# Second recurrent layer: score levels joined four blocks at a time, products of 192 columns

## The chip, the cores and the metric

The kernel runs on one core of a Trainium2 chip. The metric is the device time of one execution in microseconds (us), lower is better; the time of a kernel is the median of its runs.

## What is computed

Two transformer blocks over 256 tokens of width 1024. The first block has two layers, a gated delta rule layer and then the HGRN2 layer that this case is about; the second block is a sliding-window attention with an MLP. The HGRN2 layer, cut to its core (16 heads of 128 features, chunks of 32 tokens in the reference):

```
q_raw, f_raw, i_in, z = split(x @ w_in, 4)
f = lower_bound + (1 - lower_bound) * sigmoid(f_raw);  q = silu(q_raw);  k = 1 - f;  logf = log(f)
b = cumsum(logf)                                       # inside a chunk
attn[t, s] = sum_d q[t, d] * k[s, d] * exp(b[t, d] - b[s, d])        for s <= t
o_t  = (q_t * exp(b_t)) @ state + attn @ v
state = state * exp(b_last) + (k * exp(b_last - b))^T @ v
out = (rms_norm(o) * silu(z)) @ w_out
```

So the score of a query t and a key s is a sum over features of q times k times the product of the forget gates f between the two tokens. Everything is float32 in and out.

## The kernel before

**Dense products.** The weights are streamed in units of 512 KB: SyncE loads a unit into `raw`, ScalarE rounds it to the high half (`whi`, L1042), GpSimd subtracts to get the low half (`wlo`, L468 and L469), and TensorE multiplies high by high, high by low and low by high (`three`, L489; lines L492, L493 and L494). In the HGRN2 layer a unit is one call of `wide_unit` (24 matmuls of 256 columns). Two units each make the forget gates, the queries, the values and the output gates of a pair of heads, so that a pair takes eight units, and the eight pairs 64.

**Steps.** Each engine runs its own copy of the loop `for g in range(HG_STEPS)`, one unit to a step, the first 64 steps for the eight pairs and ten more in which the units of the output projection are multiplied. What belongs to pair p is done at fixed offsets r = g - 8 p: its four kinds of projections at r = 0 to 7, its scores at r = 4 to 12, its output at r = 13 to 17. So at g = 8 p + 5, for one, pair p begins its scores while pair p - 1 (r = 13) makes its outputs. Within a step TensorE first multiplies the unit, then does the score work, then the product across the tile halves, the output product (`hg_out`) and the sum of squares (L892, at r = 15, behind a wait on `hg_yg`). The order is written out by hand, and an engine does its instructions in that order; there is no scheduler.

**Scores.** A tile has 128 tokens; two heads times two tiles make four score tiles (u = 0 to 3). Level s (1, 2, 4, 8, 16, 32, 64) takes the pairs of neighbouring blocks of s tokens: queries in the odd block, keys in the even one. The queries and keys lie in `QK`. The queries start as q times f (`hg_gate`, L1905). For each level:

- TensorE (`hg_levels`, L829) multiplies all 128 keys of a tile by the 64 queries in odd blocks, four matmuls of 64 columns (L846). A float32 matmul is two instructions in the trace, so they are 8 records. At level 1 four matmuls of 128 columns with the plain queries are added (L844), for the diagonal.
- VectorE (`level`, L1908) waits for these, multiplies queries and keys by the decays of the next level in one instruction of 512 elements (L1913), picks the blocks that belong to this level out of PSUM into the score tile `AA` by a masked copy of 256 elements (L1921, COPY_PREDICATED; at level 1 a copy of the diagonal too, L1918), and halves the list of decays by a reduction (L1924).

Level k of pair p is at r = 4 + k. At r = 12 come two matmuls of 128 columns across the two tiles (L855) and their copy to `CR` (L1940); at r = 13 `hg_out` (L868 to L870); at r = 14 ScalarE squares the outputs (L1378) and VectorE then multiplies them by norm gain and gate into `yg` (L1945); at r = 15 TensorE sums the squares (L892). ScalarE turns them into a root at r = 16, and VectorE finishes at r = 16 and 17.

On VectorE `yg` of pair p - 1 stands in the same step (g = 8 p + 6) behind level 2 of pair p; every linked instruction of VectorE waits for the one before it to end (`link`, `settle`).

The loop on VectorE, and what it calls at r = 5 to 14:

```
for p in range(HH // 2):
    r = g - 8 * p
    if r == 4:
        hg_gate(p)
    if 5 <= r < 12:
        level(p, r - 4)
...
    if r == 14:
        vec.wait_ge(hg_sq, p + 1)
```

Of the kernel before, what the change touches and what calls it, by code (L numbers as in the profile page):

```python
# [5 lines left out]
F32 = mybir.dt.float32  # L6
# [6 lines left out]
P = 128  # L13
# [26 lines left out]
C_DIST = C_PICK + len(LEVELS) * P // 2  # L40
# [11 lines left out]
HG_STEPS = 4 * HH + SKEW  # L52
FIRST_YA = 4 * GH
# [83 lines left out]
def build(nc, a, consts, out):  # L137
    with ExitStack() as ctx:
# [34 lines left out]
        pick = {s: con[:, C_PICK + 64 * i:C_PICK + 64 * (i + 1)].bitcast(I32) for i, s in enumerate(LEVELS)}  # L173
# [29 lines left out]
        with ExitStack() as ph:  # L203
            fth = sb("fth", [P, 2 * T], stack=ph)
            q0 = sb("q0", [P, 2, 2 * T], stack=ph)
            QK = sb("QK", [P, 2, 2, 2 * T], stack=ph)
# [34 lines left out]
        SB = [ctx.enter_context(nc.psum_tensor(f"bank{i}", [P, 512], F32)) for i in range(4)]  # L241
# [86 lines left out]
        hg_gated = sem("hg_gated")  # L328
        hg_level_mm = sem("hg_level_mm")
        hg_level = sem("hg_level")  # L330
# [150 lines left out]
        def _(pe):  # L481
# [328 lines left out]
            def hg_unit(par, which, i, t):  # L810
                return QK[:, par, which, i * T + t * P:i * T + (t + 1) * P]

# [16 lines left out]
            def hg_levels(p, k):  # L829

                par, s = p % 2, LEVELS[k - 1]
                if k == 1:
                    pe.wait_ge(hg_gated, p + 1)
                    if p > 0:
                        pe.wait_ge(hg_cross, p)
                        pe.wait_ge(hg_picked, 7 * p)
                else:
                    pe.wait_ge(hg_level, 7 * p + k - 1)
                    pe.wait_ge(hg_picked, 7 * p + max(k - 2, 1))
                for i in range(2):  # L840
                    for t in range(NT):
                        u = 2 * i + t
                        if k == 1:
                            pe.matmul(SB[0][:, u * P:(u + 1) * P], hg_unit(par, 1, i, t), q0[:, par, i * T + t * P:i * T + (t + 1) * P],  # L844
                                      start=True, stop=True)
                        last = pe.matmul(SB[k % 2][:, u * 64:(u + 1) * 64], hg_unit(par, 1, i, t), even_odd(hg_unit(par, 0, i, t), s, 1),  # L846
                                         start=True, stop=True)
                last.then_inc(hg_level_mm, 1)

            def hg_across(p):  # L850

                pe.wait_ge(hg_level, 7 * p + 7)
# [1263 lines left out]
```

## Time and profile before

| | before |
|---|---|
| median of 3 runs | 1030.72 us (1030.56 to 1031.1) |
| the profiled execution | 1031.01 us |
| its span in the trace | 1029.2 us, 18128 instructions |
| TensorE busy | 987.0 us (96%), 7200 matmul records |
| VectorE, ScalarE, GpSimd busy | 424.4, 502.9 and 669.4 us |
| granted TensorE clock, mean | 0.993 |

The span is 1.8 us shorter than the time of the same execution; the rest lies outside the trace. Busy shares are of the whole span. A matmul record's duration contains the pipeline through the array, so that the records of a row overlap: what a matmul costs is the distance from its start to the next one's start. Engine names: PE is TensorE, PEld its weight loads, DVE VectorE, ACT ScalarE, POOL GpSimd.

### The profile page before, as it was taken

What the parts mean: (1) busy time and instruction counts of PE and PEld (TensorE: products, weight loads), DVE (VectorE), ACT (ScalarE), POOL (GpSimd) and SP (SyncE); (2) the same over time, 40 slices, a digit from 0 to 9 for tenths busy, and PEclk for the clock granted to TensorE, in tenths of its full rate; (3) what the DMA queues carried; (4) which work ended last, traced back from release to release, by engine and by line L of the source; (5) the groups of instructions that cost most, each with busy time, mean ns of one, the idle gap of its engine ahead of it and who ended that gap; (6) DMA issues with size and microseconds to landing.
All of it is one profiled execution on the core that took longest, in us unless ns stands there. A gap on an engine that the chain in (4) does not pass through costs nothing.

```text
span 1029.2 us, 18128 instructions
## 1 busy us (share of the span) xinstructions
PE 987.0 (96%) x7200; PEld 924.1 (90%) x7200; DVE 424.4 (41%) x748; ACT 502.9 (49%) x705; POOL 669.4 (65%) x476
## 2 busy tenths in 40 slices
PE   4999999999999999999999999999997989999996
PEld 4899999999998889999999999888886779998884
DVE  2457653376433342444444444425557262221003
ACT  3675332573225556454465545456636625654330
POOL 3995535466444797855665666659673369889981
PEclk9999999999999999999999999999998999999998
DMA  7989757759523565644444444455552046656631
GB/s 186 213 197 130 133 100 83 143 103 106 126 98 123 174 204 166 182 123 128 139 124 124 124 142 133 131 179 174 171 168 62 20 145 203 190 182 190 204 119 41
DMA packets 131100, 146.23 MB, mean 142 GB/s; under 512 B 11006, under 2 KB 95688, under 8 KB 131016
## 3 DMA queue, kind: packets, MB, share of 16 engines
q1 hardware_dynamic: 127448, 140.06, 52.8%
q10 hardware_dynamic: 3568, 5.01, 1.5%
q8 instruction: 57, 0.93, 0.4%
q14 instruction: 27, 0.22, 0.1%
HBM read 144.00 MB, written 1.05 MB: 141 GB/s over the span
## 4 chain that ended last, share of the span: by engine, by line
PE 84%; DVE 5%; POOL 3%; issue 3%; DMA 3%; ACT 2%; SPq 1%; DVEq 0%; ACTq 0%; POOLq 0%
PE dense L492 21%; PE dense L494 21%; PE dense L493 21%; PE bank L846 4%; DMA raw<-in_w_in_even_dram 3%; PE bank L750 2%; PE bank L745 2%; POOL wlo L469 2%; PE bank L749 2%; POOL wlo L468 1%; PE bank L844 1%; PE bank L961 1%; PE bank L892 1%; PE dense L561 1%; DVE cv L1604 1%
## 5 line engine op out<-in xcount | busy, mean ns | idle before, releaser
L468 POOL TENSOR_TENSOR wlo<-raw,whi 128x512 fp32r<-128x512 f32 x200 | 260.2, 1301 | 287.9 <-ACT whi L1042 287.7
L1042 ACT ACTIVATE whi<-raw 128x1024 fp32r<-128x1024 f32 x264 | 276.4, 1058 | 327.2 <-PE dense L494 272.3
L469 POOL TENSOR_TENSOR wlo<-raw,whi 128x512 fp32r<-128x512 f32 (+1 forms) x264 | 412.6, 1570 | 27.9 <-ACT whi L1042 27.7
L492 PE MATMUL dense<-x_hi,whi 128*128 128x256 f32 x1232 | 360.9, 293 | 6.9 <-POOL wlo L469 2.3
L494 PE MATMUL dense<-x_hi,wlo 128*128 128x256 f32 x1232 | 349.1, 283 | 0.0
L493 PE MATMUL dense<-x_lo,whi 128*128 128x256 f32 x1232 | 349.1, 283 | 0.0
L492 PEld LDWEIGHTS dense<-x_hi,whi 128*128 128x128 f32 x1232 | 236.9, 192 | 11.1 <-issue 4.6
L493 PEld LDWEIGHTS dense<-x_lo,whi 128*128 128x128 f32 x1232 | 236.9, 192 | 1.8 <-issue 1.7
L494 PEld LDWEIGHTS dense<-x_hi,wlo 128*128 128x128 f32 x1232 | 236.4, 192 | 0.0
L492 PE MATMUL dense<-whi,ya_hi 128*128 128x512 f32 x192 | 77.7, 405 | 0.7 <-DVE ya_lo L2024 0.7
L494 PE MATMUL dense<-whi,ya_lo 128*128 128x512 f32 x192 | 75.0, 390 | 0.0
L493 PE MATMUL dense<-wlo,ya_hi 128*128 128x512 f32 x192 | 74.9, 390 | 0.0
L1913 DVE TENSOR_TENSOR QK<-QK,bank 128x512 f32<-128x512 f32 x48 | 33.0, 688 | 94.8 <-PE bank L846 94.8
L846 PE MATMUL bank<-QK 128*128 128x64 f32 x448 | 58.8, 265 | 0.0
L846 PEld LDWEIGHTS bank<-QK 128*128 128x128 f32 x448 | 57.1, 192 | 0.3
L1032 ACT ACT_TABLE_LOAD x32 | 41.1, 1283 | 6.3 <-issue 4.6
L1604 DVE SCALAR_TENSOR_TENSOR cv<-dense,colA,cv 128x255 f32<-128x255 f32 (+2 forms) x72 | 34.7, 481 | 22.8 <-ACT cv L1123 20.3
L492 PEld LDWEIGHTS dense<-whi,ya_hi 128*128 128x128 f32 x192 | 36.1, 188 | 8.6 <-DVE ya_lo L2024 1.1
L494 PEld LDWEIGHTS dense<-whi,ya_lo 128*128 128x128 f32 x192 | 36.0, 188 | 7.8
L493 PEld LDWEIGHTS dense<-wlo,ya_hi 128*128 128x128 f32 x192 | 36.2, 188 | 7.2 <-issue 0.5
L492 PE MATMUL dense<-whi,x_hi 128*128 128x256 f32 (+1 forms) x144 | 40.9, 284 | 0.0
L493 PE MATMUL dense<-wlo,x_hi 128*128 128x256 f32 (+1 forms) x144 | 40.6, 282 | 0.0
(294 smaller groups left out, 1471.6 us busy)
## 6 DMA issues: line engine op xcount, KB each, us to landing
raw<-in_w_in_odd_dram SPq DMA_DIRECT2D x64, 512.0 KB, 3.7
raw<-in_w_in_even_dram SPq DMA_DIRECT2D x32, 512.0 KB, 10.7
raw<-in_w_in_even_dram SPq DMA_DIRECT2D x64, 256.0 KB, 4.6
raw<-in_mlp_w_up_dram SPq DMA_DIRECT2D x32, 512.0 KB, 4.0
raw<-in_mlp_w_down_dram SPq DMA_DIRECT2D x32, 512.0 KB, 4.7
raw<-in_w_out_even_dram SPq DMA_DIRECT2D x16, 512.0 KB, 3.7
raw<-in_w_pl_gate_dram SPq DMA_DIRECT2D x16, 512.0 KB, 4.5
raw<-in_w_out_odd_dram SPq DMA_DIRECT2D x16, 512.0 KB, 3.8
```

The costliest lines, as they stand in the source:

```text
L468: pool.tensor_tensor(wlo[:, slot, 0:half], unit_slot(u)[:, 0:half], whi[:, slot, 0:half].bitcast(F32), ALU.subtract)
L469: pool.tensor_tensor(wlo[:, slot, first:2 * half], unit_slot(u)[:, first:2 * half], whi[:, slot, first:2 * half].bitcast(F32), ALU.subtrac ...
L492: pe.matmul(out_, lh, rh, start=start, stop=False, skip_group_check=True)
L493: pe.matmul(out_, lh, rl_, start=False, stop=False, skip_group_check=True)
L494: return pe.matmul(out_, ll, rh, start=False, stop=stop, skip_group_check=True)
L745: last = pe.matmul(A[:, o], unit(LT[:, g, :], u), unit(XN[:, g, :], u), start=True, stop=True)
L749: pe.matmul(B[:, u * 64:(u + 1) * 64], unit(XT[:, g, :], u), even_odd(unit(EL[:, g, :], u), lv, 0), start=True, stop=True)
L846: last = pe.matmul(SB[k % 2][:, u * 64:(u + 1) * 64], hg_unit(par, 1, i, t), even_odd(hg_unit(par, 0, i, t), s, 1), start=True, stop=True)
L1032: act.preload_act_table_set(name)
L1042: act.activation(whi[:, u % NSPL, :], unit_slot(u), ACT.Copy).then_inc(hi_done, 1)
L1604: link(vec.scalar_tensor_tensor(o, bank[:, i * T:(i + 1) * T - back], colA[:, w:w + 1], o, ALU.mult, ALU.add), conv_done if back == 3 else ...
L1913: vec.tensor_tensor(qk, qk, both_decays(p, s), ALU.mult).then_inc(hg_level, 1)
```

## The change

The blocks are joined four at a time instead of two at a time. For s = 1, 4 and 16 (`HG_BLOCKS`, at r = 6, 8 and 10) four neighbouring blocks of s tokens become one of 4 s. Six block pairs lie within four blocks; each needs its own decay on the query. `hw` holds, for each group of four, eight columns of blocks, of which the middle six are the right-hand side of one matmul of 192 columns (`hg_blocks`). So a pair of heads has four matmuls of 128 columns for the diagonal (r = 5), three times four of 192 (r = 6, 8, 10) and four of 64 for the halves (r = 11). The matmuls of r = 7 and r = 9 are gone. Banks 0 and 1 of PSUM become one tensor `bank01`.

On VectorE a block stage has ten instructions (six at s = 16), where each of two levels had a product, a pick and a reduction: the queries for the next stage (384 elements, then 256 and 128 for the extra variants, `hg_variants`), the keys (256 elements twice), and three picks of 384, 256 and 128 elements, each with a mask of runs of 3 s, 2 s and s out of 6 s; then two reductions. ScalarE gets a copy of 128 elements three times for each pair (`hg_move`). The mask table is 192 columns wider. Below are the added lines; what they replace (`hg_levels`, `level`, `both`, `both_decays`) stands in the listing above.

```
+HG_BLOCKS = (6, 8, 10)
...
+        pick = {s: con[:, C_PICK + 192 * i:C_PICK + 192 * (i + 1)].bitcast(I32) for i, s in enumerate((1, 4, 16))}
+        pick_half = con[:, C_PICK + 3 * 192:C_DIST].bitcast(I32)
...
+            def hg_diagonal(p):
+                pe.wait_ge(hg_q, p + 1)
+                if p > 0:
+                    pe.wait_ge(hg_cross, p)
+                for u in range(4):
+                    last = pe.matmul(SB[0][:, u * P:(u + 1) * P], tokens_of(hk, p % 2, u // 2, u % 2), tokens_of(q0, p % 2, u // 2, u % 2),
+                                     start=True, stop=True)
+                last.then_inc(hg_level_mm, 1)
+            def hg_blocks(p, n):
+                s = 4 ** n
+                pe.wait_ge(hg_ranked, 5 * p + n + 1)
+                pe.wait_ge(hg_picked, 5 * p + n + 1)
+                for u in range(4):
+                    six = hw[:, n % 2, u * T:(u + 1) * T].rearrange("p (m c) -> p m c", c=8 * s)[:, :, s:7 * s]
+                    last = pe.matmul(low_banks[:, u * T:u * T + 192], tokens_of(hk, p % 2, u // 2, u % 2), six, start=True, stop=True)
+                last.then_inc(hg_level_mm, 1)
+            def hg_halves(p):
+                pe.wait_ge(hg_ranked, 5 * p + 4)
+                pe.wait_ge(hg_picked, 5 * p + 4)
+                for u in range(4):
+                    last = pe.matmul(SB[0][:, u * 64:(u + 1) * 64], tokens_of(hk, p % 2, u // 2, u % 2), tokens_of(q0, p % 2, u // 2, u % 2)[:, 64:P],
+                                     start=True, stop=True)
+                last.then_inc(hg_level_mm, 1)
+            def hg_across(p):
+                pe.wait_ge(hg_ranked, 5 * p + 5)
+                pe.wait_ge(hg_picked, 5 * p + 5)
                 for i in range(2):
...
+                    last = pe.matmul(SB[0][:, i * P:(i + 1) * P], tokens_of(hk, p % 2, i, 0), tokens_of(q0, p % 2, i, 1), start=True, stop=True)
                 last.then_inc(hg_cross_mm, 1)
...
+            def hg_move(p, n):
+                s = 4 ** n
+                act.wait_ge(hg_ranked, 5 * p + n + 1)
+                if n > 0:
+                    act.wait_ge(hg_level_mm, 5 * p + n + 1)
+                act.activation(ranked(p, n + 1)[:, :, :, 0:s], hw[:, n % 2, :].rearrange("p (m b c) -> p m b c", b=2, c=8 * s)[:, :, :, 0:s],
+                               ACT.Copy).then_inc(hg_moved, 1)
+                settle(hg_moved)
...
+            def pairs(p, s):
+                link(vec.tensor_reduce(decays(p, 2 * s), decays(p, s).rearrange("p (n t) -> p n t", t=2), AX_X, ALU.mult))
+            def spread(f, n):
+                return f.unsqueeze(len(f.shape)).broadcast_to([*f.shape, n])
+            def hg_variants(p, n):
+                s = 4 ** n
+                eight = hw[:, n % 2, :].rearrange("p (n c r) -> p n c r", c=8, r=s)
+                f = decays(p, s).rearrange("p (n t) -> p n t", t=4)
+                next_two = hw[:, n % 2, :].rearrange("p (n h c r) -> p n h c r", h=2, c=4, r=s)[:, :, :, 2, :]
+                link(vec.tensor_tensor(next_two, eight[:, :, 4:6, :], spread(f[:, :, 1:3], s), ALU.mult))
+                return vec.tensor_tensor(eight[:, :, 3, :], eight[:, :, 6, :], spread(f[:, :, 1], s), ALU.mult)
             def hg_gate(p):
                 vec.wait_ge(hg_decay, 2 * p + 2)
                 vec.wait_ge(hg_q, p + 1)
+                link(vec.tensor_tensor(ranked(p, 0), q0[:, p % 2, :].rearrange("p (m b r) -> p m b r", b=2, r=1),
+                                       decays(p, 1).rearrange("p (m b r) -> p m b r", b=2, r=1), ALU.mult))
+                link(hg_variants(p, 0), hg_ranked)
+                pairs(p, 1)
+                pairs(p, 2)
+            def hg_diagonal(p):
+                vec.wait_ge(hg_level_mm, 5 * p + 1)
                 if p - 1 > 0:
...
+                    vec.wait_ge(hg_o, p - 1)
+                vec.copy_predicated(four(AA[:, p % 2, :]), all4(ident).bitcast(I32), four(SB[0])).then_inc(hg_picked, 1)
                 settle(hg_picked)
...
+            def hg_blocks(p, n):
+                s, par = 4 ** n, p % 2
+                f = decays(p, s).rearrange("p (m b t) -> p m b t", b=2, t=4)
+                three = hw[:, n % 2, :].rearrange("p (m b c) -> p m b c", b=2, c=8 * s)[:, :, :, s:4 * s]
+                if n > 0:
+                    vec.wait_ge(hg_level_mm, 5 * p + n + 1)
+                link(vec.tensor_tensor(ranked(p, n + 1)[:, :, :, s:4 * s], three, spread(f[:, :, :, 0], 3 * s), ALU.mult))
+                if n < 2:
+                    vec.wait_ge(hg_moved, 3 * p + n + 1)
+                    link(hg_variants(p, n + 1))
+                vec.wait_ge(hg_level_mm, 5 * p + n + 2)
+                keys = hk[:, par, :].rearrange("p (n t r) -> p n t r", t=2, r=s)[:, :, 0, :]
+                link(vec.tensor_tensor(keys, keys, spread(decays(p, s).rearrange("p (n t) -> p n t", t=2)[:, :, 1], s), ALU.mult))
+                keys = hk[:, par, :].rearrange("p (n t r) -> p n t r", t=2, r=2 * s)[:, :, 0, :]
+                if n == 2:
+                    vec.wait_ge(hg_moved, 3 * p + 3)
+                link(vec.tensor_tensor(keys, keys, spread(decays(p, 2 * s).rearrange("p (n t) -> p n t", t=2)[:, :, 1], 2 * s), ALU.mult), hg_ranked)
+                if n == 0:
                     free("qf", p)
+                a = AA[:, par, :].rearrange("p (u m c) -> p u m c", u=4, c=4 * s)
+                got = low_banks[:, :].rearrange("p (u c) -> p u c", u=4)[:, :, 0:192].rearrange("p u (m c) -> p u m c", c=6 * s)
+                mask = pick[s].rearrange("p (m c) -> p m c", c=6 * s).unsqueeze(1).broadcast_to([P, 4, 32 // s, 6 * s])
+                link(vec.copy_predicated(a[:, :, :, s:4 * s], mask[:, :, :, 0:3 * s], got[:, :, :, 0:3 * s]))
+                link(vec.copy_predicated(a[:, :, :, 2 * s:4 * s], mask[:, :, :, 3 * s:5 * s], got[:, :, :, 3 * s:5 * s]))
+                link(vec.copy_predicated(a[:, :, :, 3 * s:4 * s], mask[:, :, :, 5 * s:6 * s], got[:, :, :, 5 * s:6 * s]), hg_picked)
+                if n < 2:
+                    pairs(p, 4 * s)
+                    if n == 0:
+                        pairs(p, 8)
+                    else:
+                        pairs(p, 32)
+            def hg_halves(p):
+                par = p % 2
+                vec.wait_ge(hg_level_mm, 5 * p + 5)
+                f = decays(p, 64).rearrange("p (i t h) -> p i t h", i=2, t=2)
+                k = hk[:, par, :].rearrange("p (i c) -> p i c", i=2)[:, :, 0:64]
+                q = q0[:, par, :].rearrange("p (i c) -> p i c", i=2)[:, :, P + 64:T]
+                link(vec.tensor_tensor(k, k, spread(f[:, :, 0, 1], 64), ALU.mult))
+                link(vec.tensor_tensor(q, q, spread(f[:, :, 1, 0], 64), ALU.mult), hg_ranked)
+                o = AA[:, par, :].rearrange("p (u c) -> p u c", u=4)[:, :, 64:P]
+                link(vec.copy_predicated(o, pick_half.unsqueeze(1).broadcast_to([P, 4, 64]), SB[0][:, 0:256].rearrange("p (u c) -> p u c", u=4)), hg_picked)
```

VectorE's instructions before, from level 1 of a pair (r = 5) to the first instruction of level 3 (r = 7). `QK` are queries and keys, `AA` the score tiles, `con` the masks, `bank` PSUM:

```order
L1913 TENSOR_TENSOR QK<-QK,dense 128x2x256 [waits hg_level_mm,hg_cross]
L1918 COPY_PREDICATED AA<-con,bank 128x512 [waits hg_o,hg_level]
L1921 COPY_PREDICATED AA<-con,bank 128x256 [waits vec_chain]
L1924 TENSOR_REDUCE bank<-dense 128x256 [waits hg_picked]
L1913 TENSOR_TENSOR QK<-QK,bank 128x2x128x2 [waits vec_chain,hg_level_mm]
L1921 COPY_PREDICATED AA<-con,bank 128x128x2 [waits hg_level]
L1924 TENSOR_REDUCE bank<-bank 128x128 [waits hg_picked]
L1945 SCALAR_TENSOR_TENSOR yg<-bank,colB,szo 128x512 [waits hg_z,hg_sq,vec_chain]
L1913 TENSOR_TENSOR QK<-QK,bank 128x2x64x4 [waits hg_level_mm,hg_yg]
```

The same place in the changed program, r = 5 (its first row) and all of r = 6. `hw` are the query blocks, `hk` the keys:

```order
L1957 COPY_PREDICATED AA<-con,bank 128x512 [waits hg_o,hg_level_mm,hg_cross]
L1967 TENSOR_TENSOR hw<-hw,dense 128x64x2x3 [waits hg_picked]
L1939 TENSOR_TENSOR hw<-hw,bank 128x64x4 [waits hg_moved,vec_chain]
L1940 TENSOR_TENSOR hw<-hw,bank 128x32x4 [waits vec_chain]
L1973 TENSOR_TENSOR hk<-hk,dense 128x256 [waits hg_level_mm,vec_chain]
L1977 TENSOR_TENSOR hk<-hk,bank 128x128x2 [waits vec_chain]
L1983 COPY_PREDICATED AA<-con,bank 128x128x3 [waits hg_ranked]
L1984 COPY_PREDICATED AA<-con,bank 128x128x2 [waits vec_chain]
L1985 COPY_PREDICATED AA<-con,bank 128x128 [waits vec_chain]
L1927 TENSOR_REDUCE bank<-bank 128x64 [waits hg_picked]
L1927 TENSOR_REDUCE bank<-bank 128x32 [waits vec_chain]
L2026 SCALAR_TENSOR_TENSOR yg<-bank,colB,szo 128x512 [waits hg_z,hg_sq,vec_chain]
```

Between the wait for the matmuls (`hg_level_mm`, at L1913 before and L1973 now) and `yg` there stood three instructions; now seven stand there.

TensorE in the changed program around the same place: the score matmuls of r = 6 (pair p), the dense matmuls of the step after (`L503` to `L505`, of which the first three stand here), and the sum of squares of pair p - 1:

```order
L857 MATMUL bank<-hw,hk 128x192 [waits hg_picked,hg_ranked]
L857 MATMUL bank<-hw,hk 128x192 x3
L503 MATMUL dense<-x_hi,whi 128x256 [waits lo_done]
L504 MATMUL dense<-x_lo,whi 128x256
L505 MATMUL dense<-x_hi,wlo 128x256
...
L914 MATMUL bank<-sqo,con 128x512 [waits hg_yg]
```

Before, four matmuls of 64 columns of r = 7 stood between that dense step and the sum of squares; now it follows the dense step at once.

## Rows read from the trace of the kernel before

**Rows 1.** The page: busy time, TensorE's granted clock in 40 slices, the chain.

```profile
PE 987.0 (96%) x7200; PEld 924.1 (90%) x7200; DVE 424.4 (41%) x748; ACT 502.9 (49%) x705; POOL 669.4 (65%) x476
...
PEclk9999999999999999999999999999998999999998
...
PE 84%; DVE 5%; POOL 3%; issue 3%; DMA 3%; ACT 2%; SPq 1%; DVEq 0%; ACTq 0%; POOLq 0%
```

**Rows 2.** Stage view: us, busy (instructions) by engine, clock, DMA share, GB/s.

```profile
core 0: us, PE busy (x) PEld busy (x) DVE busy (x) ACT busy (x) POOL busy (x), PEclk, DMA share, GB/s
410.00:665.00 255.00, 255.00 (x2089) 249.35 (x2088) 113.44 (x203) 132.07 (x163) 163.71 (x130) 1.00 0.45 135
536.00:568.77 32.77, 32.77 (x278) 32.29 (x276) 14.59 (x26) 17.68 (x23) 20.30 (x16) 1.00 0.43 129
```

**Rows 3.** Waits from 405 to 665 us: who for whom, us, times, longest.

```profile
DVE QK L1913 <- PE bank L846: 127.1, 56, 4.2
POOL wlo L468 <- ACT whi L1042: 91.3, 60, 3.6
ACT sqo L1378 <- issue: 9.5, 6, 1.6
```

**Rows 4.** TensorE's timeline, r = 5 to 8 of one pair: start, duration.

```profile
538.95 0.39 PE L844 MATMUL bank<-q,QK 128*128 128x128 f32 x2
...
540.69 0.44 PE L868 MATMUL bank<-AA,vtok 128*128 128x128 f32 x2
...
542.00 0.36 PE L492 MATMUL dense<-x_hi,whi 128*128 128x256 f32 x1
...
544.95 1.00 PE L846 MATMUL bank<-QK 128*128 128x64 f32 x8
545.76 0.36 PE L492 MATMUL dense<-x_hi,whi 128*128 128x256 f32 x1
545.97 0.28 PE L493 MATMUL dense<-x_lo,whi 128*128 128x256 f32 x1
...
548.72 1.00 PE L846 MATMUL bank<-QK 128*128 128x64 f32 x8
549.56 1.08 PE L892 MATMUL bank<-sqo,con 128*128 128x512 f32 x2
550.07 0.68 PE L492 MATMUL dense<-x_hi,whi 128*128 128x256 f32 x1
550.59 0.28 PE L493 MATMUL dense<-x_lo,whi 128*128 128x256 f32 x1
```

**Rows 5.** VectorE's timeline over the same steps.

```profile
541.68 0.74 DVE L1918 COPY_PREDICATED AA<-con,bank 128x512 f32<-128x512 int32 x1
542.46 0.74 DVE L1921 COPY_PREDICATED AA<-con,bank 128x256 f32<-128x256 int32 x1
543.23 0.70 DVE L1924 TENSOR_REDUCE bank<-dense 128x256 f32<-128x512 f32 x1
545.99 0.69 DVE L1913 TENSOR_TENSOR QK<-QK,bank 128x512 f32<-128x512 f32 x1 [2.06 <-PE bank L846]
546.72 0.76 DVE L1921 COPY_PREDICATED AA<-con,bank 128x256 f32<-128x256 int32 x1
547.51 0.43 DVE L1924 TENSOR_REDUCE bank<-bank 128x128 f32<-128x256 f32 x1
547.97 0.75 DVE L1945 SCALAR_TENSOR_TENSOR yg<-bank,colB,szo 128x512 f32<-128x512 f32 x1
...
550.55 0.44 DVE L1921 COPY_PREDICATED AA<-con,bank 128x256 f32<-128x256 int32 x1
```

**Rows 6.** VectorE's groups by shape: count, busy us, mean ns.

```profile
L1998 DVE SCALAR_TENSOR_TENSOR lg<-con,dense 128x384 f32<-128x384 f32 x16 | 8.9, 553 | 8.9 <-PE dense L942 8.5
L1940 DVE COPY CR<-bank 128x256 f32<-128x256 f32 x8 | 3.4, 425 | 12.4 <-PE bank L855 12.4
L1924 DVE TENSOR_REDUCE bank<-bank 128x64 f32<-128x128 f32 x8 | 2.4, 299 | 0.3
L1924 DVE TENSOR_REDUCE bank<-bank 128x32 f32<-128x64 f32 x8 | 1.9, 232 | 0.3
```

**Rows 7.** All engines, 780 to 783 us: a stop of TensorE ended by VectorE.

```profile
780.93 1.42 DVE L1970 SCALAR_TENSOR_TENSOR qa<-dense,root 128x512 f32<-128x512 f32 x2 [0.16 <-DVE rsum L2017]
...
782.40 1.22 PE L941 MATMUL dense<-ka,qa 64*128 64x256 f32 x3 [2.91 <-DVE qa L1970]
```

**Rows 8.** ScalarE's timeline, r = 4 and r = 14.

```profile
533.08 0.58 ACT L1353 ACTIVATE q<-dense 128x512 f32<-128x512 f32 x1
...
542.33 0.60 ACT L1378 ACTIVATE sqo<-bank 128x512 f32<-128x512 f32 x1 [1.58 <-issue]
```

More of the change, by code:

```diff
@@ L240, in build @@
         DB = [[ctx.enter_context(nc.psum_tensor(f"dense{i}{j}", [P, 512], F32)) for j in range(2)] for i in range(2)]
-        SB = [ctx.enter_context(nc.psum_tensor(f"bank{i}", [P, 512], F32)) for i in range(4)]
+        low_banks = ctx.enter_context(nc.psum_tensor("bank01", [P, 1024], F32))
+        SB = [low_banks[:, 0:512], low_banks[:, 512:1024]]
+        SB += [ctx.enter_context(nc.psum_tensor(f"bank{i}", [P, 512], F32)) for i in (2, 3)]
         raw_ready = [sem(f"raw_ready{i}") for i in range(NRAW)]
@@ L327, in build @@
         hg_z = sem("hg_z")
-        hg_gated = sem("hg_gated")
+        hg_ranked = sem("hg_ranked")
+        hg_moved = sem("hg_moved")
         hg_level_mm = sem("hg_level_mm")
-        hg_level = sem("hg_level")
         hg_picked = sem("hg_picked")
@@ L807, in _, with tokens_of @@
             layer_tail(0)
-            def hg_unit(par, which, i, t):
-                return QK[:, par, which, i * T + t * P:i * T + (t + 1) * P]
+            def tokens_of(buf, par, i, t):
+                return buf[:, par, i * T + t * P:i * T + (t + 1) * P]
             def hg_dense(g):
@@ L827, in hg_dense @@
                     last.then_inc(split_used, 1)
[L829 to L847, printed above, removed]
+            def hg_diagonal(p):
[6 more added lines that the diff above has]
+                last.then_inc(hg_level_mm, 1)
@@ L853, in hg_across @@
-                pe.wait_ge(hg_picked, 7 * p + 6)
+                pe.wait_ge(hg_ranked, 5 * p + 5)
+                pe.wait_ge(hg_picked, 5 * p + 5)
                 for i in range(2):
-                    last = pe.matmul(SB[0][:, i * P:(i + 1) * P], hg_unit(p % 2, 1, i, 0), hg_unit(p % 2, 0, i, 1), start=True, stop=True)
+                    last = pe.matmul(SB[0][:, i * P:(i + 1) * P], tokens_of(hk, p % 2, i, 0), tokens_of(q0, p % 2, i, 1), start=True, stop=True)
                 last.then_inc(hg_cross_mm, 1)
@@ L1398, in _ @@
                 split_until(min(FIRST_SPLIT[("hg_f", 0, 0)] + g + 1 + AHEAD, FIRST_SPLIT[("pl", 1, 0)]))
+                for p in range(HH // 2):
+                    r = g - 8 * p
+                    if r + 1 in HG_BLOCKS:
+                        hg_move(p, HG_BLOCKS.index(r + 1))
                 for p in range(HH // 2):
@@ L1933, in _ @@
                         hg_gate(p)
-                    if 5 <= r < 12:
-                        level(p, r - 4)
+                    if r == 5:
+                        hg_diagonal(p)
+                    if r in HG_BLOCKS:
+                        hg_blocks(p, HG_BLOCKS.index(r))
+                    if r == 11:
+                        hg_halves(p)
                 for p in range(HH // 2):
@@ L2081, in shape_constants @@
         out[:, C_NEG + n * P:C_NEG + (n + 1) * P] = np.where(below, -1, 0)
-        out[:, C_PICK + n * 64:C_PICK + (n + 1) * 64] = below.T.reshape(P, P // (2 * s), 2, s)[:, :, 1, :].reshape(P, 64)
         if s == 1:
             out[:, C_NEG1T:C_NEG1T + P] = np.where(below.T, -1, 0)
+    for n, s in enumerate((1, 4, 16)):
+        same = np.arange(P)[:, None] // (4 * s) == np.arange(P // (4 * s))[None, :]
+        block = np.arange(P) // s % 4
+        rows = np.stack([block == b for b in (0, 0, 0, 1, 2, 1)], 1)
+        mask = (same[:, :, None] & rows[:, None, :])[:, :, :, None].repeat(s, 3)
+        out[:, C_PICK + 192 * n:C_PICK + 192 * (n + 1)] = mask.reshape(P, 192)
+    out[:, C_PICK + 3 * 192:C_DIST] = np.arange(P)[:, None] < 64
     key = np.arange(2 * P)[None, :]
```

47 lines of the change are left out of this document (14 added, 33 removed).

## Prediction

> **What bounds the kernel now.** I read the page first. TensorE is busy 96% of the span and makes 84% of the chain that ended last, at a granted clock of 0.9 or more of full speed in every slice [rows 1]; VectorE is busy 41%. Then I read the stretch that the change touches. From 410 to 665 us TensorE is busy for all of 255.00 us at a clock of 1.00, which is the 2.4 GHz level, while VectorE is busy for 113 [rows 2]. One pair of heads takes 32.77 us and TensorE has no gap in it [rows 2]. The waits of this stretch say the same: TensorE waits for nobody, VectorE waits 127.1 us in total for the score matmuls [rows 3]. So what TensorE no longer does comes off the end, microsecond for microsecond, as long as no wait of TensorE takes its place. Two questions decide: how much shorter is TensorE's own work, and does VectorE, now slack, stay ahead of each place where TensorE waits for it?
>
> **TensorE's own work.** Only the distance between starts is read. Level 1 with the diagonal runs from 538.95 to 540.69: 1.74 us for 8 records of 128 columns and 8 of 64. The output product that follows takes from 540.69 to 542.00, 12 records of 128 columns, 0.109 us each. So the 8 records of 64 columns cost 1.74 - 8 x 0.109 = 0.87 us. The group of level 3 takes 548.72 to 549.56, 0.84 us, where a sum of squares follows. The group of level 2 starts at 544.95; the dense matmul after it starts at 545.76 and the next at 545.97, and two dense matmuls are some 0.12 apart, so the group costs 545.97 - 544.95 - 0.12 = 0.90 us with the change of kind at its edges, which is 0.105 a record and 0.06 for the edges [rows 4].
>
> - Removed for each pair: the 64-column groups of r = 5 (0.87), of r = 7 (0.84) and of r = 9 (0.90). Sum 2.61 us.
> - Widened: the groups of r = 6, 8 and 10 from 64 to 192 columns. No row has 192. The nearest are 64 columns at 0.105, 128 at 0.109 and 512: the two records of the sum of squares cost 550.59 - 549.56 - 0.12 = 0.91 us with edges [rows 4], so 0.43 each without. From 64 to 128 columns nothing is added, and 512 costs in proportion to its columns: a record costs its columns or some 0.105, whichever is more. 192 columns then cost 192/512 x 0.43 = 0.16. Eight records are 8 x (0.16 - 0.105) = 0.44 us more, three groups 1.32. If the whole 0.455 of a 512-column record went by columns it would be 0.17 and 1.6 us.
> - The group of r = 11 keeps its size, and the diagonal and the product across the tiles keep theirs.
>
> Net 2.61 - 1.32 = 1.29 us for each pair, **10.3 us** for eight (bounds 8 and 11).
>
> **The new wait.** At g = 8 p + 7 TensorE sums the squares of pair p - 1 and must have `yg`. On VectorE `yg` stands behind all of pair p's stage at r = 6, and that stage cannot go on before the score matmuls of r = 6 are done. Before, these matmuls started at 544.95, VectorE's product followed at 545.99, and `yg` ended at 547.97 + 0.75 = 548.72; TensorE came to the sum at 549.56 [rows 4, 5]. That is 0.84 us to spare, just what the matmuls of r = 7 took. Now they are gone and the chain on VectorE is longer. With B for the start of the r = 6 matmuls:
>
> - TensorE comes to the sum at B + 0.81 (the old group, 544.95 to 545.76) + 0.44 (wider) + 2.96 (the dense step, 545.76 to 548.72) = B + 4.21 [rows 4].
> - VectorE starts its keys at B + 1.04 + 0.44 = B + 1.48 [rows 4, 5].
> - Two key products of 256 elements. 384 elements take 0.553 and a copy of 256 takes 0.425 [rows 6]; 512 take 0.69 [rows 5]. So some 0.155 plus 1.04 ns an element: 0.42 each, 0.84.
> - Three masked picks at s = 1. This is the dear part. Before, a pick of 256 elements took 0.74 at s = 1 and 0.76 at s = 2, but 0.44 at s = 4, and the diagonal's 512 elements, contiguous, took 0.74 [rows 5]. The mask and the bank were read in one piece in all of them; what differs is how broken the writing is. Counting elements, broken runs cost some 2.2 ns each and long runs 1.1. Counting groups of four neighbours in the score tile, each group touched costs 4.4 ns, whether one, two or four of it are written: 128 groups at s = 1, at s = 2 and for the diagonal, 64 at s = 4. The new picks write 3, 2 and 1 of each four. By elements they are 1.03 + 0.75 + 0.46, by groups 0.75 three times: 2.24 both ways. I take 2.24.
> - Two reductions, 0.30 + 0.23 [rows 6], then `yg`, 0.75 [rows 5].
> - Seven gaps of 0.03 between linked instructions, as between the rows of [rows 5]: 0.24.
>
> The sum is 0.84 + 2.24 + 0.53 + 0.75 + 0.24 = 4.60, so `yg` ends at B + 6.08. TensorE starts 0.05 us after VectorE's end where it waited for it elsewhere (780.93 + 1.42 to 782.40) [rows 7]. It starts the sum at B + 6.13 in place of B + 4.21, and stands still for **1.92 us**. This happens for the seven pairs that have one behind them, 13.4 us. Nothing earns it back: the next unit stands behind the sum on TensorE. The squares are not what is late: ScalarE made them from 542.33 [rows 8], long before.
>
> **What stays hidden.** TensorE's matmuls of r = 8 need the picks of r = 6, and those of r = 10 the picks of r = 8; two dense steps lie between, over 5.9 us, for chains of 4.6 us at most. From r = 10 to r = 11 there is one dense step: VectorE starts at 1.48, two key products 0.84, three picks at s = 16, where runs are long (0.59 + 0.44 + 0.31), gaps 0.13, ends at 3.79 against 4.21, so 0.4 us are to spare. At r = 4 VectorE now does the halves' three short ones, the query product, two variants and two reductions before the copy to `CR`. From ScalarE's query (533.08 + 0.58 [rows 8]), 1 us into a dense step, these are 0.69 + 0.42 + 0.29 + 0.70 + 0.43 and the copy 0.42, done 4.5 us into that step, where the diagonal needs it only after that step, the product across and the next step, over 6 us. ScalarE's three small copies a pair, no longer than the 0.6 us of its 512-element ones [rows 8], stand behind its unit copies; it is busy for 17.68 of 32.77 us [rows 2] and GpSimd, which waits for it, for 20.30. The wider mask table is loaded once, far ahead. All of this at nothing.
>
> **Sum.** -10.3 + 13.4 = +3.1 us. Against the profiled execution, 1031.01, that is 1034.1; the median of the runs shown is 0.3 lower, so I predict 1033.8.
>
> **Rivals.**
>
> - *Cheap picks.* If short runs of three and one cost what long ones do and the pair of two as well, the picks are 0.59 + 0.44 + 0.31 = 1.34, the stop is 1.02 us, seven of them 7.1, and the time is 1030.7 - 3.2 = 1027.5. Against it: 0.74 and 0.76 in every one of eight pairs at s = 1 and 2. For it: no row has three of four. Chance 0.16.
> - *Only touches of a line count.* Here a pick pays extra only where a single element of four is written: 0.59 + 0.44 + 0.74 = 1.77, the stop 1.45, seven of them 10.1, the net -0.2 and the time 1030.5. Rows speak against it, since two of four already cost 0.74 where four cost 0.44 [rows 5]. The Trainium skill (SBUF — State Buffer, section on the DMA port swizzle, its note on "cachelines") states this rule: lines of 16 bytes, full bandwidth with two or more accesses to a line, a penalty with one. By that rule the old picks at s = 1 and 2 would have been full speed; the trace disagrees with its 0.74 against 0.44. Chance 0.16.
> - *A second stop, or dear columns.* If the picks at s = 16 also cost 2.24, because their masks and banks are now read in pieces, r = 11 is late by 0.5 us in eight pairs (4 us), the first stop grows by some 0.3 (2 us) for the same reason, and 192 columns may cost the upper bound (2.3 us). This goes to slower from 0.4 us of extra on VectorE at r = 10 on; the time would be about 1040. Chance 0.12.
> - *No stop.* If VectorE were ahead after all, the 10.3 us would stand alone: 1020.4. For that, 1.9 of the 4.6 us that I count on VectorE would have to be missing, more than cheap picks can give. Chance 0.04.
>
> **How the numbers follow.** The forecast has 0.52. What a measurement of this kernel can tell from no change is about 0.2%, or 2 us. The forecast's own spread (stop 1.7 to 2.1, gain 9.5 to 10.7) is +1.2 to +5.2, of which I put 0.07 within 2 us. Slower: 0.45 + 0.12 = 0.57; same: 0.07 + 0.16 = 0.23; faster: 0.16 + 0.04 = 0.20. The range goes from the cheap picks to just short of the second stop: 1027 to 1038.5, which leaves out the case without a stop and most of the last but one.
>
> **What would show it.** In the changed profile TensorE should wait for VectorE's `yg` seven times, some 1.9 us each, and for nothing else between 405 and 665 us. A group of eight 192-column records should take some 1.3 us to the next dense matmul. The picks at s = 1 should add up to 2.2 us, those at s = 4 and 16 to 1.3. The period of a pair should be 32.77 - 1.29 + 1.92 = 33.4 us. The prediction is wrong if that wait is missing or below 1.4 us, or if TensorE stops at r = 11.

## The result

The changed kernel took 1040.7 us (median of 6 runs, 1035.2 to 1043.3) beside 1030.6 us for the kernel before; the ratio is 1.0088, 95% interval 1.0064 to 1.0111. Measured once more, beside the experiments below, it was 1038.9 us beside 1030.5, ratio 1.0075 (1.0059 to 1.0091). So it is slower by some 8 to 10 us. I had forecast slower by 3 us and a range up to 1038.5. The profiled execution took 1039.84 us, its span is 1038.0 us.

Waits from 400 to 680 us in the changed kernel (who waits for whom, us in total, times, longest). Before, TensorE stood in no row of this stretch [rows 3]:

```profile
DVE hk L1973 <- PE bank L857: 73.0, 24, 5.7
...
PE bank L914 <- DVE yg L2026: 14.0, 7, 2.0
ACT L1054 <- PE bank L914: 11.6, 7, 2.4
DVE hk L2000 <- PE bank L865: 11.2, 8, 1.7
```

TensorE's timeline over r = 6 and 7 of one pair, the counterpart of [rows 4], start and duration:

```profile
514.27 1.47 PE L857 MATMUL bank<-hw,hk 128*128 128x192 f32 x8
515.44 0.41 PE L503 MATMUL dense<-x_hi,whi 128*128 128x256 f32 x1
...
518.32 0.28 PE L505 MATMUL dense<-x_hi,wlo 128*128 128x256 f32 x1
520.59 1.12 PE L914 MATMUL bank<-sqo,con 128*128 128x512 f32 x2 [1.99 <-DVE yg L2026]
521.15 0.68 PE L503 MATMUL dense<-x_hi,whi 128*128 128x256 f32 x1
```

VectorE's timeline over the same time, the counterpart of [rows 5]:

```profile
515.84 0.42 DVE L1973 TENSOR_TENSOR hk<-hk,dense 128x256 f32<-128x256 f32 x1 [3.42 <-PE bank L857]
516.30 0.42 DVE L1977 TENSOR_TENSOR hk<-hk,bank 128x256 f32<-128x256 f32 x1
516.87 0.75 DVE L1983 COPY_PREDICATED AA<-con,bank 128x384 f32<-128x384 int32 x1
517.65 0.74 DVE L1984 COPY_PREDICATED AA<-con,bank 128x256 f32<-128x256 int32 x1
518.43 0.72 DVE L1985 COPY_PREDICATED AA<-con,bank 128x128 f32<-128x128 int32 x1
519.18 0.56 DVE L1927 TENSOR_REDUCE bank<-bank 128x64 f32<-128x128 f32 x2
519.78 0.75 DVE L2026 SCALAR_TENSOR_TENSOR yg<-bank,colB,szo 128x512 f32<-128x512 f32 x1
```

This is the wait that the prediction named, at its place and seven times, 2.00 us each. VectorE starts 1.57 us after the matmuls, `yg` ends 6.26 us after them, and TensorE starts the sum 0.06 us later. The three picks take 0.75, 0.74 and 0.72 us for 384, 256 and 128 elements.

What the prediction did not have shows in the granted clock. Two pairs in the view by stages (us, busy by engine, clock, DMA share, GB/s), one after the other, and then the 8 us around a stop, 2 us each:

```profile
506.21:539.77 33.56, 31.57 (x254) 30.89 (x252) 18.60 (x40) 18.63 (x26) 20.25 (x17) 1.00 0.41 126
539.77:574.90 35.13, 33.13 (x253) 32.05 (x252) 18.61 (x40) 18.61 (x26) 20.26 (x17) 0.95 0.40 120
```

```profile
620.00:622.00 2.00, 0.88 (x8) 0.68 (x6) 1.90 (x4) 0.94 (x1) 0.58 (x1) 1.00 0.14 17
622.00:624.00 2.00, 1.12 (x3) 0.61 (x3) 1.86 (x5) 0.60 (x2) 1.81 (x2) 0.71 0.70 244
624.00:626.00 2.00, 2.00 (x8) 1.48 (x7) 0.19 (x1) 1.02 (x1) 0.68 (x1) 0.50 0.29 24
626.00:628.00 2.00, 2.00 (x18) 2.00 (x17) 0.00 (x0) 1.94 (x4) 0.00 (x0) 0.94 0.64 240
```

After a stop TensorE's clock stands at 0.50, the 1.2 GHz level, for somewhat over 3 us, and the pair takes 35.13 us instead of 33.56. This happened after two of the seven stops. The stop is the only time of such a pair in which TensorE is not busy (31.57 of 33.56 us).

All runs can be compared on one stretch, from the first score matmul of pair 0 to the last sum of squares. It is in the rows that group a line's instructions (durations in ns, first and last start), of the kernel before and then of the changed one:

```profile
L844 PE MATMUL bank<-q,QK x64: 272/275/324, 410.1 to 638.7; 128*128 128x128 f32 x64
L892 PE MATMUL bank<-sqo,con x16: 590/592/648, 451.3 to 676.5; 128*128 128x512 f32 x16
```

```profile
L846 PE MATMUL bank<-q,hk x64: 272/275/275, 412.9 to 647.4; 128*128 128x128 f32 x64
L914 PE MATMUL bank<-sqo,con x16: 590/697/1223, 453.4 to 686.7; 128*128 128x512 f32 x16
```

Before, 410.1 to 676.5 is 266.4 us; now 412.9 to 686.7 is 273.8 us, **7.4 us** of the 8.8 us between the two profiled executions. The rest lies outside: the stretch begins 2.8 us later, as the clock was also down for nearly 7 us from 25.5 us on in this execution, and the attention stage took 1.4 us less.

### The profile page after: what moved, and what is told of

Its sections match the earlier page's. It is cut to its first block, busy times and chain, and to the rows that moved or that the text cites. A ratio compares the mean times of both kernels' runs of the same rounds, so it can differ in the third digit from the quotient of the medians.

```text
span 1038.0 us, 17909 instructions
## 1 busy us (share of the span) xinstructions
PE 984.7 (95%) x7008; PEld 919.2 (89%) x7008; DVE 452.3 (44%) x852; ACT 510.6 (49%) x729; POOL 668.9 (64%) x476
## 4 chain that ended last, share of the span: by engine, by line
PE 85%; DVE 8%; ACT 2%; DMA 2%; issue 1%; SPq 0%; POOL 0%; DVEq 0%; ACTq 0%
PE dense L503 22%; PE dense L505 21%; PE dense L504 21%; PE bank L857 3%; PE bank L761 2%; PE bank L756 2%; DMA raw<-in_w_in_even_dram 2%; PE bank L760 2%; PE bank L914 1%; PE bank L983 1%; PE dense L572 1%; PE bank L846 1%; PE bank L865 1%; DVE x_lo L1543 1%; DVE yg L2026 1%
## 5 line engine op out<-in xcount | busy, mean ns | idle before, releaser
L503 PE MATMUL dense<-x_hi,whi 128*128 128x256 f32 x1232 | 364.5, 296 | 8.7 <-POOL wlo L480 4.7
L505 PE MATMUL dense<-x_hi,wlo 128*128 128x256 f32 x1232 | 351.4, 285 | 0.0
L503 PEld LDWEIGHTS dense<-x_hi,whi 128*128 128x128 f32 x1232 | 239.4, 194 | 13.2 <-issue 3.8
L504 PEld LDWEIGHTS dense<-x_lo,whi 128*128 128x128 f32 x1232 | 239.4, 194 | 2.3 <-issue 2.2
L505 PEld LDWEIGHTS dense<-x_hi,wlo 128*128 128x128 f32 x1232 | 239.0, 194 | 0.0
L503 PE MATMUL dense<-whi,ya_hi 128*128 128x512 f32 x192 | 77.7, 405 | 0.7 <-DVE ya_lo L2105 0.7
L505 PE MATMUL dense<-whi,ya_lo 128*128 128x512 f32 x192 | 74.9, 390 | 0.0
L503 PEld LDWEIGHTS dense<-whi,ya_hi 128*128 128x128 f32 x192 | 36.1, 188 | 8.6 <-DVE ya_lo L2105 1.1
L505 PEld LDWEIGHTS dense<-whi,ya_lo 128*128 128x128 f32 x192 | 36.1, 188 | 7.8
L503 PE MATMUL dense<-whi,x_hi 128*128 128x256 f32 (+1 forms) x144 | 40.9, 284 | 0.0
L505 PE MATMUL dense<-whi,x_lo 128*128 128x256 f32 (+1 forms) x144 | 40.5, 282 | 0.0
L503 PE MATMUL dense<-whi,yb_hi 128*128 128x512 f32 x96 | 38.2, 398 | 0.1
L2135 DVE TENSOR_TENSOR xtok<-xtok,dense 128x512 f32<-128x512 f32 x4 | 2.7, 687 | 81.5 <-PE dense L505 81.4
```

The source lines that it names most:

```text
L503: pe.matmul(out_, lh, rh, start=start, stop=False, skip_group_check=True)
L504: pe.matmul(out_, lh, rl_, start=False, stop=False, skip_group_check=True)
L505: return pe.matmul(out_, ll, rh, start=False, stop=stop, skip_group_check=True)
```

## The experiments

**The spread and the order on VectorE.** My theory (A): VectorE's order makes the stop, the stop makes the clock fall. The rival (B): the 192-column matmuls make it fall. First the changed kernel again, and with `yg` ahead of the block stage:

```
             for g in range(HG_STEPS):
+                for p in range(HH // 2):
+                    r = g - 8 * p
+                    if r == 14:
+                        vec.wait_ge(hg_sq, p + 1)
+                        vec.wait_ge(hg_z, p + 1)
+                        vec.scalar_tensor_tensor(yg[:, :], SB[3][:, :], colB[:, HGRNG:HGRNG + 1], szo[:, p % 2, :], ALU.mult, ALU.mult).then_inc(hg_yg, 1)
+                        settle(hg_yg)
                 for p in range(HH // 2):
                     r = g - 8 * p
                     if r == 4:
                         hg_gate(p)
...
-                    if r == 14:
-                        vec.wait_ge(hg_sq, p + 1)
-                        vec.wait_ge(hg_z, p + 1)
-                        vec.scalar_tensor_tensor(yg[:, :], SB[3][:, :], colB[:, HGRNG:HGRNG + 1], szo[:, p % 2, :], ALU.mult, ALU.mult).then_inc(hg_yg, 1)
-                        settle(hg_yg)
```

> The changed kernel once more, beside the next three. Theory A: seven stops of TensorE of 2.0 us each at the sum of squares, and after some of them the granted clock falls for a few us at a price of about 1.6 us each (in the profile of the changed kernel after two of seven). Then the times are a ladder: about 1035 us with no fall and 1.6 us more for each, up to about 1046. Theory B: the spread has another source (the transfers, the 192-column matmuls themselves); then the times do not follow the number of stops with a lower clock, and falls are also seen away from the stops.

Measured: 1038.9 us (1035.4 to 1041.0), stretch 273.8 us, seven stops of 2.0 us, two falls of the clock after them. In the six runs the time and the mean clock do not go together closely enough to count falls: one run of 1038.3 us had a clock of 0.991, two of 1035.4 and 1035.8 had 0.988. The ladder of the expectation failed at its foot: this profiled execution took 1035.4 us with two falls in the stretch, the first one 1039.8 us with two as well. The 4.4 us between them lie outside: the stretch began at 410.2 us in place of 412.9, and the attention stage took 103.2 us in place of 105.0. So the times alone do not count falls.

> The changed kernel with VectorE's yg moved ahead of the block stage in the same step; nothing else. Theory A (order on VectorE makes the stop, the stop makes the clock fall): no stop, no fall, a pair takes 32.77 - 1.36 = 31.4 us, so the time is the kernel before less 8 x 1.36 = 10.9 us, about 1020, with the small spread of the kernel before. Theory B (192-column matmuls or their operands trouble the clock): the stops go (14 us less than the changed kernel) but falls stay, so 1021 to 1027 with a wide spread.

Measured: **1014.5 us** (1013.4 to 1018.7), ratio 0.9856 (0.9838 to 0.9874). TensorE waits for nobody in the stretch, its clock stays up, and the stretch is 254.9 us. VectorE's timeline, r = 6:

```profile
505.06 0.75 DVE L2012 SCALAR_TENSOR_TENSOR yg<-bank,colB,szo 128x512 f32<-128x512 f32 x1 [1.28 <-ACT sqo L1410]
505.85 0.56 DVE L1967 TENSOR_TENSOR hw<-hw,dense 128x384 f32<-128x384 f32 x1
506.44 0.42 DVE L1939 TENSOR_TENSOR hw<-hw,bank 128x256 f32<-128x256 f32 x1
506.89 0.29 DVE L1940 TENSOR_TENSOR hw<-hw,bank 128x128 f32<-128x128 f32 x1
508.57 0.42 DVE L1973 TENSOR_TENSOR hk<-hk,dense 128x256 f32<-128x256 f32 x1 [1.40 <-PE bank L857]
```

`yg` fits into time in which VectorE was waiting anyway: 1.40 us are still left behind it. The stretch gives TensorE's own gain without any stop: 266.4 - 254.9 = **11.5 us, 1.44 for each pair**. That leaves, of the changed kernel's 273.8, 18.9 us for the stops and the clock: 7 x 2.24 and two falls at 1.6. It fits the period, 32.77 - 1.44 + 2.24 = 33.57 against 33.56. The median is 5 us below the expected 1020; where these lie is taken up below.

Why does a stop that the profile gives as 2.00 us cost 2.24? TensorE's rows of this kernel, from the score matmuls of r = 6 to the matmuls behind the sum, beside those of the changed kernel above:

```profile
507.00 1.47 PE L857 MATMUL bank<-hw,hk 128*128 128x192 f32 x8
...
511.05 0.28 PE L505 MATMUL dense<-x_hi,wlo 128*128 128x256 f32 x1
511.18 1.02 PE L914 MATMUL bank<-sqo,con 128*128 128x512 f32 x2
511.63 0.68 PE L503 MATMUL dense<-x_hi,whi 128*128 128x256 f32 x1
```

Without a stop the sum starts 4.18 us after the score matmuls, 0.15 us before the dense record ahead of it ends. With the stop it starts 6.32 us after them, 1.99 us after that record ended. From start to start the stop is thus 2.14 us. The next dense matmul follows the sum's start at 0.56 us in place of 0.45, which is 0.11 more. Why it comes later after a stop is not shown.

**The length of the stop.** Two kernels shorten it, by moving work of the first block stage behind `yg`:

```
-                if n < 2:
+                if n == 1:
                     pairs(p, 4 * s)
-                    if n == 0:
-                        pairs(p, 8)
-                    else:
-                        pairs(p, 32)
+                    pairs(p, 32)
...
+                for p in range(HH // 2):
+                    if g - 8 * p == 6:
+                        third_pick(p, 0)
+                        pairs(p, 4)
+                        pairs(p, 8)
```

The first kernel moves the two reductions (`pairs`) alone; the second also takes the third pick at s = 1 out of the stage and makes it here (`third_pick`).

> The changed kernel with the two reductions of the first block stage moved behind yg. The chain ahead of yg is shorter by 0.28 x 2 + gaps = 0.6 us, the stop should be 1.4 us instead of 2.0: 7 x 0.6 = 4.2 us less than the changed kernel without falls, about 1030.5 us. Theory A says falls get rarer as the stop gets shorter, theory B that they are as many as before.

> As the one before, and the third pick at s = 1 (128 elements, 0.72 us in the profile) is also behind yg. If a pick costs by groups of four touched, the stop shrinks by 0.72 + 0.03 more to 0.65 us, the time to about 1025.3 us. If the 0.72 were an accident of this place (GpSimd at work beside it), moving it would change its duration.

Measured: 1028.4 us (1025.0 to 1032.8), ratio 0.9982 (0.9968 to 0.9995), and 1023.7 us (1019.9 to 1027.9), ratio 0.9932 (0.9913 to 0.9951), each about 2 us below what was expected. The waits for `yg` in the two:

```profile
PE bank L914 <- DVE yg L2023: 9.8, 7, 1.4
```

```profile
PE bank L914 <- DVE yg L2032: 4.5, 7, 0.6
```

The stops are 1.40 and 0.64 us as expected; the stretches are 266.4 and 261.1 us, that is 11.5 and 6.2 above the one without a stop, or 1.64 and 0.89 for each stop: 0.24 us above its idle in both. No fall of the clock lies in either stretch. The third pick took 0.73 us in its new place too, so its price is no accident of the old one.

**Stops without the change.** The kernel before, with extra copies on VectorE ahead of `yg`, four in the first kernel and six in the second:

```
+                        for _ in range(4):
+                            link(vec.tensor_copy(spare[:, :], SB[3][:, :]))
                         vec.scalar_tensor_tensor(yg[:, :], SB[3][:, :], colB[:, HGRNG:HGRNG + 1], szo[:, p % 2, :], ALU.mult, ALU.mult).then_inc(hg_yg, 1)
```

> The kernel before (64-column matmuls, its own picks) with four extra copies of 512 elements on VectorE ahead of yg, 4 x 0.72 = 2.88 us, of which 0.84 us is the room it had: seven stops of TensorE of 2.04 us at the same place as in the changed kernel. If the stop is all that matters (theory A), each costs its idle and the 0.24 us of restart that the changed kernel showed, 7 x 2.28 = 16 us: 1046.5 us without falls of the clock, and falls at 1.6 us each after some of the seven stops, so a spread up to 1058. If falls belong to the 192-column matmuls (theory B), the time is 1046.5 with the spread of the kernel before.

> The same with six copies: stops of 3.48 us, 7 x 3.7 = 26 us, 1056.5 us without falls. Theory A expects more falls than with 2.04 us, up to one for each stop (11 us more, 1068); theory B none.

Measured: 1046.9 us (1044.6 to 1050.0), stretch 286.1; and 1066.9 us (1063.5 to 1068.4), stretch 305.5. The waits for `yg` of the first and the second:

```profile
PE bank L893 <- DVE yg L1948: 13.7, 7, 2.0
```

```profile
PE bank L893 <- DVE yg L1948: 23.9, 7, 3.4
```

One stop of the second kernel in the view by stages:

```profile
640.00:644.00 4.00, 2.29 (x21) 2.15 (x19) 3.79 (x7) 1.54 (x2) 2.87 (x4) 1.00 0.26 80
644.00:646.00 2.00, 0.30 (x1) 0.30 (x2) 1.90 (x4) 0.00 (x0) 1.16 (x1) 0.79 0.27 102
646.00:648.00 2.00, 2.00 (x5) 0.97 (x5) 1.09 (x3) 0.20 (x1) 0.00 (x0) 0.50 0.68 221
648.00:650.00 2.00, 2.00 (x16) 2.00 (x16) 0.00 (x0) 1.96 (x3) 0.00 (x0) 0.86 0.11 41
```

With 64-column matmuls only, the clock fell after three of seven stops of 2.0 us (at 488, 560 and 632 us) and at all seven of 3.4 us, sometimes just before the stop ended. What a fall costs is read from two pairs of the first kernel, from one sum of squares to the next, with a fall and without:

```profile
487.81:524.26 36.45, 34.50 (x274) 33.75 (x274) 17.35 (x31) 17.68 (x22) 20.28 (x17) 0.95 0.40 115
524.26:559.20 34.94, 32.98 (x274) 32.37 (x274) 17.37 (x31) 17.68 (x22) 20.27 (x17) 1.00 0.41 123
```

A stop costs 34.94 - 32.77 = 2.17 us here, for an idle of 1.96, and a fall 1.5. So the first stretch is 19.7 us longer than before: 15.2 for seven stops and 4.5 for three falls. The second is 39.1 us longer: 7 x (3.41 + 0.21) = 25.3, and 13.8 for seven falls. Two of these lasted twice as long, the one at the last stop and the one at the first, which is shown here:

```profile
454.00:461.00 7.00, 6.05 (x23) 5.02 (x24) 2.27 (x5) 3.73 (x4) 0.41 (x1) 0.51 0.27 79
```

Counted as nine of the usual length they cost 1.5 us each, as in the first kernel. Theory B is out: falls come with stops, whatever the score matmuls are. The expected time held for the second kernel. For the first it held in part by luck: 1046.5 us was expected without falls, the profiled execution took 1046.9 with three, and its attention stage was 3.3 us shorter than before.

**Cover without a longer wait.** The changed kernel with useless matmuls where those of r = 7 stood:

```
+                if 8 < g < 4 * HH and g % 8 == 7:
+                    for u in range(4):
+                        pe.matmul(pair_of("vz", g // 8)[1][:, u * 64:(u + 1) * 64], ident, zero[:, :], start=False, stop=False, skip_group_check=True)
                 if g < 4 * HH:
```

> The changed kernel with four matmuls of 64 columns that add zero to a bank, ahead of the dense step between the r = 6 matmuls and the sum of squares, where the matmuls of r = 7 stood; nothing else moves. The idle before the sum should shrink by 0.84 to 1.16 us and the pair should take as long as before, so without falls the time is that of the changed kernel without falls, about 1035. Theory A: fewer falls with the shorter idle, median 1035 to 1037. Theory B: no change, median 1039.

Measured: 1035.0 us (1030.6 to 1038.3, 12 runs), ratio to the kernel before 1.0054 (1.0035 to 1.0073). The idle is 8.1 us in seven stops, 1.45 for the first and 1.11 to 1.12 for the others, none with a fall, and the stretch is 271.1 us: about what the changed kernel's would be without its two falls (273.8 - 3.2 = 270.6). So more work on TensorE made the profiled stretch 2.7 us shorter, through the clock. The medians were taken beside different runs of the kernel before; of their ratios to it, 1.0054 against 1.0075 and 1.0088 for the changed kernel, the intervals overlap.

**The edit alone on the kernel before, and twice on the changed one.**

> The kernel before with yg moved ahead of level 2 on VectorE, the edit of e1 alone. There is no stop to take away, so nothing changes: 1030.5 us, within 0.1%. If it is faster by several us, part of what e1 gained is not the stop of the changed kernel.

Measured: 1027.3 us (1024.0 to 1031.3), ratio 0.9987 (0.9964 to 1.0009), which includes no change. Its stretch is 266.4 us, the same as before. That it can read 1024 is no gain of the edit: the unchanged kernel had runs from 1024.7 to 1031.8 us beside it. The difference lies in the attention stage, here from 755 to 855 us in the kernel before and then in this one:

```profile
755.00:855.00 100.00, 85.89 (x607) 76.35 (x607) 58.40 (x107) 51.89 (x123) 50.58 (x35) 0.95 0.29 91
```

```profile
755.00:855.00 100.00, 89.51 (x661) 80.26 (x660) 53.03 (x107) 55.51 (x126) 56.09 (x38) 0.98 0.34 103
```

TensorE waits often there, and the clock was down for nearly 7 us and again for over 3 us in the one, once for over 3 us in the other. From the row product before the attention to the one after it I read 106.4 and 100.0 us.

> The kernel of e1 once more. Its stretch from the first score matmul to the last sum of squares was 11.5 us shorter than before, its median 16 us. Theory: only the 11.5 us are the change's, the rest is where falls of the clock happen to lie in the attention stage, in both kernels; then the median here lies 10 to 16 us below the kernel before on this chip, and the stretch is 254.9 us again. Rival: the whole 16 us belong to the edit; then the difference is 16 us again wherever the kernel before lies.

Measured: 1018.1 us (1015.9 to 1019.3) beside 1030.4, ratio 0.9873 (0.9856 to 0.9890); stretch 254.8 us; attention stage 104.9 us against 100.3 in the profile of the first time. So 11.5 us are shown as the change's with this order. The remaining 1 to 5 us of the medians go with the attention stage, as far as the profiled executions show: for the kernel before against the first time with `yg` ahead it is 11.5 in the stretch and 6.1 there.

**The stop taken away on TensorE's side.**

```
-                    if r == 15:
+                    if r == 16:
                         pe.wait_ge(hg_yg, p + 1)
```

> The changed kernel with TensorE's sum of squares one step later (r = 16, behind the r = 8 matmuls), VectorE's order as in the changed kernel. If the stop is only the place at which TensorE asks for yg, it goes here too: no wait for yg, the stretch up to the transposes of the layer's end as short as in e1 (269.3 us against 280.8 before), time about 1015 to 1020. Rival: ScalarE, which now waits for the sum some 4 us longer before its root and its next unit copy, becomes the wait; then TensorE waits for wlo at some steps and part of the 11 us is gone.

Measured: 1021.7 us (1016.3 to 1023.7), ratio 0.9898 (0.9874 to 0.9922). No wait for `yg` is left and the clock stays up; from the first score matmul to the transposes at the layer's end it takes 271.8 us, against 269.2 with `yg` first and 280.9 before. So the stop goes, but the time is not quite as short as expected. Of the 2.6 us, 2.0 are the rival in small, one wait near the layer's end (up to 680.8 us), seen in the waits from 405 to 700 us:

```profile
PE dense L503 <- POOL wlo L480: 2.0, 1, 2.0
```

## Why the prediction was right and wrong

- **What bounds the kernel**: right. TensorE was the bound in the stretch, and both the gain and the stops came through to the end.
- **TensorE's own work**: mechanism right, size low. I had 1.29 us for a pair, the runs show 1.44, 11.5 us in place of 10.3. The group of eight records of 192 columns cost 1.30 us by the measure of [rows 4] (514.27 to 515.69, less 0.12), not 1.34, which is 0.12 for three groups. The rest shows at the sum: with the matmuls of r = 7 gone and no stop, the dense matmul behind it starts 0.45 us after it (511.18 to 511.63) in place of 0.51 [rows 4].
- **The new wait**: right in place, count and cause. I had `yg` at B + 6.08 and it came at 6.26: VectorE started 0.09 later, the gaps added up to 0.36 where I had 0.24 (one of 0.15 stood ahead of the first pick; and seven of 0.03 would have been 0.21), and the picks cost 2.21 where I had 2.24.
- **"and stands still for 1.92 us ... 13.4 us"** is the step that failed: the price of a stop was too low, and the clock had no term. My 1.92 was the delay of the sum, B + 6.13 in place of B + 4.21. Measured it is B + 6.32 in place of B + 4.18, 2.14 us. The restart adds 0.11, for which I had nothing. So a stop costs 2.24 by the stretch, seven of them 15.7 us. And I left out that TensorE's clock can fall after one: two falls, 3.2 us, in each of the two profiles of the changed kernel. In the stretch that is 18.9 us against my 13.4. Less 11.5 for the gain it is the +7.4 measured, against my +3.1.
- **What lies outside the stretch** I had at nothing as well. Added to the median before, the 7.4 us alone would give 1038.0, just inside my range. The rest of the 1040.7 us lies elsewhere, in the first profile at the start (2.8 us), and the two profiles of the changed kernel differ by 4.4 us there.
- **The picks**: of the two ways to count, by groups of four touched is the one that fits: 0.75, 0.74 and 0.72 for 384, 256 and 128 elements. In these picks mask and bank are read in pieces too, so that the writing alone makes the price is shown by the old picks only (two of each four), not for one or three. By elements it would have been 1.03, 0.75 and 0.46; the sum is the same, so the forecast did not hang on it.
- **What stays hidden**: right. TensorE waits in none of the other places. The rival of a second stop at r = 11 fell (VectorE's picks at s = 16 take 0.60, 0.46 and 0.30 us and end before TensorE asks), as did those of cheap picks (0.75, 0.74 and 0.72 us at s = 1) and of no stop. The time of about 1040 that I gave the first of them is near the measured one, by a mechanism that did not happen.
- **The Trainium skill's rule** on lines of 16 bytes (SBUF — State Buffer, section on the DMA port swizzle) did not hold for masked picks: two and three accesses to a line cost as much as one. It does fit a plain product that I had not singled out. `hg_variants` at s = 1 writes single elements four apart and takes 0.62 us for 256 elements, where runs of four and more take 0.42. No run separates the writing from its broken reads of the decays. The rows (changed kernel, VectorE's groups by shape, mean ns):

```profile
L1939 DVE TENSOR_TENSOR hw<-hw,bank 128x256 f32<-128x256 f32 x16 | 6.7, 420 | 0.6
L1939 DVE TENSOR_TENSOR hw<-hw,dense 128x256 f32<-128x256 f32 x8 | 5.0, 621 | 0.3
```

**What stays open.** Why the clock falls after two or three of seven equal stops of 2.0 us, and not after the others, is not shown. The stretch explains 7.4 us; the medians differ by 8 to 10. The remaining 1 to 3 us are not measured apart. The profiles show two places outside the stretch where the clock is down. In the attention stage it is so in both kernels: the stage takes 100.0 to 106.4 us in the four profiles with the old score stage and 100.3 to 108.4 in the eight with the new one. Between 25 and 53 us it is so in five of the eight with the new one (the stretch then begins up to 2.8 us later) and in none of the four with the old one. Whether this is chance or comes with the change, for one with its wider mask table that is loaded at the start, was not tried.

## What to carry to other kernels

When work is taken from the engine that bounds a kernel, list what that work was covering: here the 0.84 us of matmuls at r = 7 were just the room that `yg` had. If what the engine then waits for needs nothing of the chain ahead of it in its queue, it goes first: one moved instruction turned +8 to +10 us into -12 to -16, and in the stretch +7.4 into -11.5. And price a stop of TensorE from start to start, with the restart, and count on the clock too where stops are as long as the 2 us here.

## What the runs showed of the hardware

- The granted clock fell to 0.50 after 2 of 7, 2 of 7 and 3 of 7 stops of 2.0 us, at 7 of 7 stops of 3.4 us, and after none of 21 stops of 1.4, 1.16 and 0.64 us (means of seven), each among otherwise unbroken matmuls. A fall of somewhat over 3 us cost 1.5 to 1.6 us; two of those at the stops of 3.4 us lasted twice as long.
- A stop cost 0.24 us above its idle at 0.64, 1.4 and 2.0 us alike in the changed kernel, and 0.21 in the kernel before. 0.15 of it is how the idle is counted, since an unbroken row starts 0.15 us before the one ahead ends; the rest is a later matmul behind the restart.
- A masked copy from PSUM costs by the groups of four neighbouring float32 it touches in its output: 0.72 to 0.75 us for 128 groups, whether one, two, three or four of each are written (with one and three, mask and source are read in pieces as well).
- Float32 matmul records with all 128 rows and columns of weights followed each other at 0.105 us for 64 columns, 0.11 for 128, 0.155 for 192 (1.30 less 0.06, by 8) and 0.43 for 512.
